# The expert router reads the raw residual, in four column strips

## What is computed

```python
def rmsnorm(x, w, eps=NORM_EPS):
    y = x * lax.rsqrt(jnp.mean(x * x, axis=-1, keepdims=True) + eps)
    return y * w
...
pg = jax.nn.softmax(hf @ w_group)          # hf = rmsnorm(h, norm_ffn_w), w_group (1024, 4)
gidx, gprob = jnp.argmax(pg), jnp.max(pg)
sub_all = jnp.einsum('btd,gde->btge', hf, w_sub)    # w_sub (4, 1024, 4)
vals, idx = lax.top_k(sub_of_group_gidx, 2)
w2 = softmax(vals) * gprob
hid = silu(hf @ w_gate[e]) * (hf @ w_up[e]) * gate ; out = hid @ w_down[e]
```

## Time and profile before

| what | value |
|---|---|
| median of 3 runs | 1477.9 us (1473.82, 1477.9, 1481.07) |
| profiled execution, its own time | 1483.33 us |
| its span, first to last instruction | 1481.5 us |
| TensorE busy | 1305.9 us, 88% |
| VectorE, ScalarE, GpSimd busy | 726.8, 410.8, 176.3 us |
| mean granted TensorE clock | 0.934 of full |
| MixOut and Experts of layer 0 | 375 to about 653 us of the span |
| MixOut and Experts of layer 1 | 1161.8 to about 1446 us of the span |

### The profile page before, as it was taken

How to read it: one execution, slowest core, us unless ns; L and a number is a source line. 1 busy time by engine, 2 the same in 40 slices (tenths; PEclk the granted TensorE clock), 3 DMA queues, 4 the chain that set the end, 5 groups by cost and what they waited for, 6 DMA issues and landing times. The chain is left out here.

```text
span 1481.5 us, 29946 instructions
## 1 busy us (share of the span) xinstructions
PE 1305.9 (88%) x11855; PEld 769.3 (52%) x11855; DVE 726.8 (49%) x1881; ACT 410.8 (28%) x1098; POOL 176.3 (12%) x247
## 2 busy tenths in 40 slices
PE   6999999998799998966999989858778699998897
PEld 3445555565366654534555545435554355755542
DVE  3445777676565311137353544368875565321123
ACT  3024445353210211133213121234546211121112
POOL 2002233222010000013021100100100001000002
PEclk9999999999898899987999999988998799799998
DMA  6150435223714899994455989899999622899925
GB/s 231 58 149 14 134 112 169 73 77 132 285 54 170 306 363 346 320 326 163 150 201 223 341 316 351 320 410 405 406 385 346 235 96 89 335 371 343 327 73 192
DMA packets 133278, 348.15 MB, mean 235 GB/s; under 512 B 22491, under 2 KB 52366, under 8 KB 124942
## 3 DMA queue, kind: packets, MB, share of 16 engines
q1 hardware_dynamic: 115906, 313.63, 59.3%
q0 software_dynamic: 4992, 17.83, 3.3%
q10 hardware_dynamic: 12236, 14.72, 3.0%
HBM read 302.61 MB, written 43.52 MB: 234 GB/s over the span
## 5 line engine op out<-in xcount | busy, mean ns | idle before, releaser
L409 PE MATMUL bank<-wring,xT 128*128 128x512 f32 x448 | 200.0, 601 | 0.0
L409 PEld LDWEIGHTS bank<-wring,xT 128*128 128x128 f32 x448 | 84.1, 192 | 100.2 <-issue 100.1
L1440 PE MATMUL bank<-wring,xT 128*128 128x512 f32 x256 | 120.1, 623 | 2.0 <-DVE xT L1360 2.0
L883 PE MATMUL bank<-xT,wring 128*128 128x512 f32 x256 | 113.5, 601 | 3.9 <-DVE hgrn_g L707 3.9
L2798 DVE STREAM_TRANSPOSE attn_k_pages<-attn_k_pages 128x1024 f32<-128x1024 f32 x64 | 77.6, 1232 | 46.5 <-DMA attn_k_pages<-cache_k 45.8
L883 PEld LDWEIGHTS bank<-xT,wring 128*128 128x128 f32 x256 | 48.7, 193 | 65.1 <-issue 59.6
L1440 PEld LDWEIGHTS bank<-wring,xT 128*128 128x128 f32 x256 | 49.6, 200 | 59.9 <-issue 59.8
L2798 DVE STREAM_TRANSPOSE wring<-wring 128x1024 f32<-128x1024 f32 x44 | 52.7, 1224 | 46.2 <-DMA wring<-cache_k 46.1
L785 DVE COPY_PREDICATED gla_att<-level_masks,bank 128x512 f32<-128x512 int32 x48 | 35.1, 731 | 71.8 <-PE bank L903 71.8
L2315 PE MATMUL bank<-xT,wring 128*128 128x512 f32 x128 | 56.9, 597 | 0.0
L903 PE MATMUL bank<-gla_qe,gla_ke 128*128 128x128 f32 x384 | 49.7, 285 | 0.0
(11 more groups left out here) (460 smaller groups left out, 2388.1 us busy)
## 6 DMA issues: line engine op xcount, KB each, us to landing
attn_k_pages<-cache_k SPq DMA_DIRECT2D x64, 512.0 KB, 7.7
wring<-cache_v SPq DMA_DIRECT2D x52, 512.0 KB, 7.7
attn_shared<-cache_v SPq DMA_DIRECT2D x44, 512.0 KB, 5.6
wring<-cache_k SPq DMA_DIRECT2D x44, 512.0 KB, 7.1
moe_wd<-moe_w_down SPq DMA_DIRECT2D x20, 1024.0 KB, 14.5
wring<-moe_w_gate SPq DMA_DIRECT2D x18, 1024.0 KB, 11.6
wring<-moe_w_up SPq DMA_DIRECT2D x18, 1024.0 KB, 15.8
wring<-a_w_in SPq DMA_DIRECT2D x16, 1024.0 KB, 10.6
```

Of the source, the lines that this page charges most:

```text
L409: last = nc.tensor.matmul(bank[:, :], xT[:, c, cols(t)], w[:, c, :], start=(c == 0), stop=(c == DC - 1))
L883: last = nc.tensor.matmul(bank[:, :], lhsT, k.xT[:, c, 0:SEQ], start=(c == 0), stop=(c == DC - 1))
L1440: last = nc.tensor.matmul(bank[:, :], k.xT[:, c, cols(t)], w[:, c, :], start=(c == 0), stop=(c == DC - 1))
```

## The change

The router's weights are scaled once per layer by the norm's weight (VectorE, in the second step), so that the router can read the residual h before it is normed: its transposes (1452) wait for the add, and take every eighth feature of the row (a step of 32 bytes), the order that the scaling used to make. The factor per token comes in the `pick`, where a copy becomes a multiply. The router's product is turned round: a chunk's router weights (padded to 32 columns) are the weights and the tokens move; four chunks stand beside each other in column strips of the array, and twice four chunks add up in them. ScalarE copies the four strips out of the bank, and one matmul with four stacked identities adds them and gives tokens by logits again. On TensorE this sum stands two chunks of the projection later, and in the last step the gather of the second tile follows it. After the loop, transposes, strips and sum of the last tile come ahead of the gather of the third. On VectorE, the last tile's copy to xT moves ahead of its inverse root and scaling. SyncE loads the norm's weight once more, by feature; GpSimd makes the padding and the stacked identities at the stage's start and waits for the scaled rows before it scatters.

```diff
--- before.py
+++ after.py
@@ -33,6 +33,7 @@
...
 EARLY, EXPERT_SLOTS = 3, 5
+STRIP = 32
 NB, STORES = 2, 6
...
@@ -1021,7 +1022,7 @@
...
         self.k, self.a, self.layer = k, a, layer
-        self.norm, self.router = sb("norm_w", [P, D]), sb("router", [P, DC, GROUPS + EXPERTS])
+        self.norm, self.strip_sum, self.strips = sb("norm_w", [P, D]), sb("strip_sum", [P, STRIP]), sb("strips", [P, P])
         by_width = lambda tile: tile[:, :, :].rearrange("p a b -> p (a b)").rearrange("p (w c f) -> p w c f", w=2, c=DC)
...
@@ -1029,6 +1030,7 @@
...
                   [late[:, i * part:(i + 1) * part].rearrange("p (c n) -> p c n", n=D) for i in range(EXPERT_SLOTS - EARLY)]
+        self.norm_column, self.router = k.cw[:, 3 + layer, :], sb("router", [P, DC, STRIP])
         self.gu_in = [sem(f"gate_up_landed{i}") for i in range(EXPERT_SLOTS)]
...
@@ -1038,6 +1040,7 @@
...
         by_feature = lambda x: x.rearrange("(p c) n -> p c n", c=DC)
+        sp.dma_start(self.norm_column, a["norm_ffn_w"][layer].rearrange("(p c) -> p c", c=DC)).then_inc(self.router_in, 16)
         sp.dma_start(self.router[:, :, 0:GROUPS], by_feature(a["moe_w_group"][layer])).then_inc(self.router_in, 16)
...
@@ -1078,14 +1081,18 @@
...
         self.big, self.more = sb("big", [P, MORE, E]), sb("more", [P, MORE])
...
 
-    def constants(self, pool, ch):
-
-        nc = self.nc
+    def constants(self, pool, ch, moe):
+
+        nc, quarter = self.nc, lambda j: self.k.ident[:, j * STRIP:(j + 1) * STRIP]
+        nc.gpsimd.memset(moe.router[:, :, GROUPS + EXPERTS:STRIP], 0.0).then_inc(self.padded, 1)
+        ch(nc.gpsimd.tensor_tensor(moe.strip_sum[:, :], quarter(0), quarter(1), ALU.add))
+        ch(nc.gpsimd.tensor_tensor(moe.strip_sum[:, :], moe.strip_sum[:, :], quarter(2), ALU.add))
+        nc.gpsimd.tensor_tensor(moe.strip_sum[:, :], moe.strip_sum[:, :], quarter(3), ALU.add).then_inc(self.padded, 1)
         nc.gpsimd.iota(self.count_i[:, :], pattern=[[1, CAP]], base=0, channel_multiplier=0).then_inc(self.made, 1)
...
@@ -1109,7 +1116,7 @@
...
 
-    def pick(self, dve, ch, i, t, bank):
+    def pick(self, dve, ch, i, t, bank, root):
 
...
@@ -1118,7 +1125,7 @@
...
         dve.wait_ge(self.logit, i + 1)
-        ch(self.nc.vector.tensor_copy(L, bank[r, t * 32:t * 32 + G + E]))
+        ch(TS(L, bank[r, t * STRIP:t * STRIP + G + E], root[r, :], None, ALU.mult))
         reduce_max(best[0], L[:, 0:G])
...
@@ -1247,10 +1254,10 @@
...
         (self.squared, self.summed, self.averaged, self.seeded, self.gated, self.turned, self.out_a, self.out_v, self.projected,
...
 
...
@@ -1272,10 +1279,11 @@
...
         routing = self.routing
-        routing.constants(pool, ch)
+        routing.constants(pool, ch, self.moe)
         self.k.order_n["gpsimd"] = ch.n
...
             pool.wait_ge(routing.slots_ready, i + 1)
+            pool.wait_ge(self.n_xs, i + 1)
             for j in range(TOPK):
...
@@ -1310,6 +1318,11 @@
...
             nc.scalar.activation(k.xT[:, half:DC, cols(t)], src, ACT.Copy).then_inc(self.n_out_a, 1)
+
+        def strips_out(i):
+            n, routing = rows(ORDER[i]), self.routing
+            act.wait_ge(routing.in_strips, i + 1)
+            nc.scalar.activation(self.moe.strips[:, 0:n], k.ps[6][:, HB - P:HB - P + n], ACT.Copy).then_inc(routing.strips_out, 1)
 
...
@@ -1322,9 +1335,11 @@
...
                 norm_out(i - 1)
+                strips_out(i - 1)
             squares(i, 1)
...
         norm_out(NT - 1)
+        strips_out(NT - 1)
 
...
@@ -1372,6 +1387,8 @@
...
             dve.wait_ge(self.n_mean, i + 1)
+            if i == NT - 1:
+                norm_out(i)
             dve.wait_ge(self.n_root, i + 1)
...
@@ -1385,6 +1402,15 @@
...
             nc.vector.tensor_copy(k.xT[:, 0:half, cols(t)], src).then_inc(self.n_out_v, 1)
+
+        def pick(i):
+            routing.pick(dve, ch, i, ORDER[i], logit_bank, self.mean[:, 5, ORDER[i]:ORDER[i] + 1])
+
+        def router_scaled():
+            dve.wait_ge(self.moe.router_in, 16 * (2 + GROUPS))
+            router = self.moe.router[:, :, 0:GROUPS + EXPERTS]
+            nc.vector.tensor_tensor(router, router, bcast(self.moe.norm_column, 2, [P, DC, GROUPS + EXPERTS]), ALU.mult)\
+                .then_inc(self.router_ready, 1)
 
...
@@ -1402,16 +1428,17 @@
...
             if i:
+                if i == 1:
+                    router_scaled()
                 norm_out(i - 1)
-                route(routing.pick, i - 1, logit_bank)
+                pick(i - 1)
             else:
...
         norm(NT - 1)
-        norm_out(NT - 1)
-        route(routing.pick, NT - 1, logit_bank)
+        pick(NT - 1)
         route(routing.slots, NT - 1, pos_bank)
...
@@ -1447,22 +1474,34 @@
...
             t = ORDER[i]
-            pe.wait_ge(self.n_xs, i + 1)
+            pe.wait_ge(self.added, 2 * i + 2)
+            by_chunk = k.h[0:rows(t), t, :].rearrange("p (q c) -> p c q", c=DC)
             for c in range(DC):
                 last = nc.tensor.transpose(k.ps[2 + c // half][:, (c % half) * P:(c % half) * P + rows(t)],
-                                           self.xs[0:rows(t), t, c * P:(c + 1) * P], k.ident[0:rows(t), 0:rows(t)])
+                                           by_chunk[:, c, :], k.ident[0:rows(t), 0:rows(t)])
             last.then_inc(self.n_turned, 1)
 
-        def logits(i):
+        def logit_strips(i):
+
             t = ORDER[i]
             if i == 0:
-                pe.wait_ge(moe.router_in, 16 * (1 + G))
+                pe.wait_ge(self.router_ready, 1)
+                pe.wait_ge(routing.padded, 2)
             pe.wait_ge(self.n_out_v, i + 1)
             pe.wait_ge(self.n_out_a, i + 1)
-            for c in range(DC):
-                last = nc.tensor.matmul(k.ps[6][0:rows(t), t * 32:t * 32 + G + E], k.xT[:, c, cols(t)], moe.router[:, c, :],
-                                        start=(c == 0), stop=(c == DC - 1))
-            last.then_inc(routing.logit, 1)
+            per = P // STRIP
+            for n in range(DC // per):
+                for j in range(per):
+                    last = nc.tensor.matmul(k.ps[6][j * STRIP:(j + 1) * STRIP, HB - P:HB - P + rows(t)], moe.router[:, n * per + j, :],
+                                            k.xT[:, n * per + j, cols(t)], start=(n == 0), stop=(n == DC // per - 1))
+            last.then_inc(routing.in_strips, 1)
+
+        def logit_sums(i):
+
+            t = ORDER[i]
+            pe.wait_ge(routing.strips_out, i + 1)
+            nc.tensor.matmul(k.ps[6][0:rows(t), t * STRIP:t * STRIP + G + E], moe.strips[:, 0:rows(t)], moe.strip_sum[:, 0:G + E],
+                             start=True, stop=True).then_inc(routing.logit, 1)
 
...
@@ -1479,9 +1518,10 @@
...
             pe.wait_ge(routing.selected, i + 1)
+            pe.wait_ge(self.n_xs, i + 1)
             return gather_tokens(nc, k.ps[0:2], self.xs, routing.select, ORDER[i], i == 0, i == NT - 1)
 
-        whole, first, second = range(DC), range(half), range(half, DC)
+        whole, first, second, third = range(DC), range(half), range(half, half + half // 2), range(half + half // 2, DC)
         turn(0)
...
@@ -1497,15 +1537,20 @@
...
             if i:
-                logits(i - 1)
+                logit_strips(i - 1)
             if i == NT - 1:
...
             project(i, 1, w[1], second)
+            if i:
+                logit_sums(i - 1)
+            if i == NT - 1:
+                gather(1)
+            project(i, 1, w[1], third)
         place(NT - 2)
-        gather(1)
+        norm_turn(NT - 1)
+        logit_strips(NT - 1)
+        logit_sums(NT - 1)
         gather(2)
-        norm_turn(NT - 1)
-        logits(NT - 1)
         gather(3)
...
```

More of the change, by code:

```diff
@@ L1080, in __init__ @@
         self.big, self.more = sb("big", [P, MORE, E]), sb("more", [P, MORE])
-        names = ("made", "cleared", "logit", "picked", "placed", "summed", "slots_ready", "selected", "counted", "sent", "gathered", "compared", "stepped", "to_exp",
+        names = ("made", "cleared", "padded", "in_strips", "strips_out", "logit", "picked", "placed", "summed", "slots_ready", "selected", "counted", "sent", "gathered", "compared", "stepped", "to_exp",
                  "exped", "blocks_ready")
-        (self.made, self.cleared, self.logit, self.picked, self.placed, self.summed, self.slots_ready, self.selected, self.counted,
+        (self.made, self.cleared, self.padded, self.in_strips, self.strips_out, self.logit, self.picked, self.placed, self.summed, self.slots_ready, self.selected, self.counted,
          self.sent, self.gathered, self.compared, self.stepped, self.to_exp, self.exped, self.blocks_ready) = (k.sem(f"{tag}_{n}") for n in names)
-    def constants(self, pool, ch):
-        nc = self.nc
+    def constants(self, pool, ch, moe):
[4 more added lines that the diff above has]
+        nc.gpsimd.tensor_tensor(moe.strip_sum[:, :], moe.strip_sum[:, :], quarter(3), ALU.add).then_inc(self.padded, 1)
```

(4 more changed lines are left out.)

## The result

The changed kernel took 1485.43 us in the median of 20 runs, the kernel before 1479.82 us in 20 runs beside it: ratio 1.004, 95% interval 1.0021 to 1.006. It is slower by 0.4%, or 5.6 us (3 to 9). The forecast was 0.26% faster. The profiled execution took 1484.43 us (span 1482.7), 0.1% under its median. That is only 1.1 us over the profiled execution of the kernel before (1483.33), so the rows of the two traces cannot hold the whole 5.6 us: they show where each path moved, and the times of the runs carry the sum.

A forecast was written before the change was run, and what follows sets the result against it. The prediction saw layer-end routing as the bound, with a path of transfers almost beside it. Limited by transfers, -1.5 us in layer 1 and -2.4 in layer 0 made -3.9: 1477.9 to 1474.0, range 1466 to 1485.

The forecast's parts named there:

- (a): Last tile's router no longer waits for the norm: pick 4.2 us earlier, 0.4 lost to gathers, routing line -3.8 in layer 1.
- (b): Router matmuls in column strips: 0.5 us against 1.86; with the gather moved in, the projection ends 0.9 us later.
- (c): Longer TensorE gap in the third pass brings a lower-clock spell: +1.0 us at the projection's end, bounds -1.3 and +2.5.
- (d): Transposing the residual loads weights at a 32-byte step: no penalty taken, upper bound +1.1 us per tile.
- (f): Transfers limit the gain: token reads land 2.5 us after the full stretch; expert 1's turn -1.5 us in layer 1, -2.4 in layer 0.
- The 3.8: Upper bound, in us, from the full transfer stretch's end to the first token read's landing; a read issued to idle engines.
- sign of being right: TensorE idle 1 to 2 us before the turn of expert 1's tokens, named as a wait on slots_x.
- the sign of being wrong: The projection ending more than 3 us later, or expert 1's turn following expert 0 with no wait.
- The shift is passed on, so that buys nothing: After expert 1's turn, weight loads follow TensorE's freed slots, passing the shift on; expert 5's earlier first weights gain nothing.
- the third rival: Transfers take the whole gain: reads need 3.8 us, clock spell doubles, +0.5 to +2 us per layer, 1479 to 1482; chance 0.2.
- The forecast's case: The routing gain arrives only as far as the transfers allow: 1471 to 1477 us; chance 0.37.

The follow-up runs named there:

- both undone: Changed kernel with the second tile's gather back behind the projection and TensorE's third-pass pause filled with unused matmuls; ratio to the kernel before 1.0001.
- the filled pause: Changed kernel with 13 unused matmuls of 224 columns where TensorE waits for the copy to xT in the third pass; ratio 0.9989.
- the second execution: Changed kernel, unedited, profiled and timed once more beside the kernel before; ratio 1.0034.
- the early weights: Changed kernel with expert 3's gate and up weights issued when the last tile's first half projection is done; ratio to the kernel before 0.9978.
- the waiting transposes: Changed kernel, but in the third pass alone the transposes wait for the scaling again; ratio to the kernel before 0.9999.
- the helps without the change: Kernel before, with expert 3's weights issued early and nine unused matmuls in the third pass's two gaps; ratio 0.9972.
- the best version: Changed kernel with the gather put back, TensorE's pause filled and expert 3's weights issued early; 1468.9 us, ratio to the kernel before 0.9914.

## Why the prediction was wrong, step by step

- **(a) was right.** The pick ends 5.2 us sooner after the projection in layer 1 and 5.8 in layer 0; 4.2 in absolute time with an add 0.7 to 0.9 later made 4.9 to 5.1. The 0.4 for the cold gathers was too small in layer 0: 32 instructions took 6.85 us at the lower clock (473.97 to 480.8), so the placement stood 1.8 us behind the pick's end (478.8).
- **(b) was right in its parts, too small in its sum.** 16 strip instructions take 0.64 us (0.5 forecast) at the upper clock and 1.08 at the lower, the two-instruction sum 0.24 to 0.4, and 0.62 at the lower clock in the third pass. The gather moved in takes 2.00 and costs the projection 1.8 (its own experiment). But the strips won only about 0.3 at the projection's end (71.9 with both undone, 72.15 to 72.2 before), where I had let them give back 1.1: without the clock the projection ends 1.5 later, not 0.9.
- **(c) failed in its size.** The stretch at 1.2 GHz grew from 3.4 to 6.8 us in both layers. Layer 0, where it had ended ahead of the fourth projection (7.13 in the earlier trace rows), now has it there too (8.21). I took +1.0 because the row near it cost 1.3; the filled pause gives 2.5 and 1.8, and the stated bound was 2.5. The projection ends 4.0 and 1.8 us later in place of 1.9 (4.05 and 2.55 in the second execution). In layer 1 the 1.8 looks like a hit, but there the kernel compared had its own costly stretch (8.40); its executions without one end at 72.2. Over three executions before and four after with TensorE's work unedited (the two kernels, the second profile and the kernels that moved weights alone) the end goes from 72.7 to 76.05 on average, 3.3 later per layer.
- **(d) was right.** Eight transposes with weights at a step of 32 bytes take 1.12 to 1.16 us where they took 1.09 to 1.11; only the 32-row tile shows more, 1.06 against 0.68. By the rule of the Trainium skill (SBUF — State Buffer, Door 1: The DMA port swizzle) crossing 16-byte lines has its penalty; it gives no size. For these loads the rows show at most 0.07 us per eight of the 128-row ones, not my upper bound of 1.1, and the measurement decides.
- **(f) failed, and here lies the sign.** I let the reads land 2.5 us after the full stretch, as if they flowed beside its end. But they are issued only once the last scatter has landed; that scatter, issued 4 to 5 us sooner, lands with the stretch all the same (8.84 us in place of 4.64), and the read takes its 3.65 after it. So where TensorE comes early enough to wait, the end of the projection fixes the turn, and not the routing; with the gather put back alone the routing still set it. The 3.8 stood in my bounds, and it was the right end, behind a stretch that itself ended later. The TensorE wait that I named as a sign of being right (1 to 2 us on slots_x) did come, 1.64 and 1.75: the path was right and its length wrong. And the sign of being wrong came too, a projection that ends more than 3 us later, in layer 0.
- **"The shift is passed on, so that buys nothing"** failed too. The experts behind the turn run on the same line of transfers: shifting 2.1 MB costs 0.6% with the turn in place. The kernel before stood on both lines at about the same time. The change shortened the one and lengthened the other, and the time follows the longer. In the changed kernel the line of transfers starts 5.8 us later over both layers (6.6 in the second execution), and 5.6 us were measured. That the two agree so closely is partly luck: by the averages under (c) it is 6.7. That all of the 5.6 goes by this line is worked out, not isolated. That starting it earlier wins the loss back is shown in two ways whose intervals lie apart from the 1.0021 to 1.006: the filled pause (0.9989; against the second set of runs, 1.0012 to 1.0055, it just overlaps) and the early weights (0.9978, apart from both), the latter with TensorE's program untouched. The gather put back (1.0018), the waiting transposes (0.9999) and both undone (1.0001) point the same way, but their intervals overlap it; and why both undone are not faster than the filled pause alone stays open.

What came true is the third rival, the transfers with the doubled clock spell, which I gave 0.2. Its 1479 to 1482 stood against 1477.9, where the measured ratio makes 1483.8, so even its own range was 2 us short: it took +2 per layer at most, and the projection's end alone brought 1.8 to 4.0. The forecast's case had looked likelier because I summed a gain of one line (2.8 us) and let the other line move by the small end of each unknown.

## What to carry to other kernels

Where two lines end within a microsecond of each other, a change must be summed on each from its own start, and what it does to the start of the other one (here a gather of 2 us and a slower clock ahead of the projection's end) counts in full. Test the slack by moving a known load (2.1 MB here) before believing it. A shortened line may show its worth only together with an edit that shortens the other: 1.004 for the change alone, 0.9978 with early weights, 0.9972 for the helps without the change, 0.9914 together.

## What was not expected of the hardware

Useless matmuls gained time. The profile's windows around the pause in layer 0 (columns as above) show the granted clock, last but two, at 0.50 right after it, while TensorE is busy throughout, and back at 1.00 only from 434:

```profile
425.00:428.00 3.00, 0.00 (x0) 0.00 (x0) 2.77 (x13) 1.70 (x4) 0.42 (x1) 0.80 0.00 0
428.00:431.00 3.00, 2.99 (x46) 2.43 (x50) 0.40 (x3) 0.28 (x1) 1.76 (x2) 0.50 0.52 195
431.00:434.00 3.00, 3.00 (x16) 1.32 (x9) 2.58 (x13) 0.00 (x0) 0.00 (x0) 0.56 0.39 160
434.00:437.00 3.00, 3.00 (x9) 1.33 (x8) 1.75 (x8) 0.93 (x3) 0.00 (x0) 1.00 0.00 0
```

With 5.19 us of matmuls in that pause the clock did not fall. Gathers go with either level: 32 gather instructions took 6.85 us in the changed kernel, where the clock fell to 0.50 within their first microsecond and stayed there, and 3.98 in the best version (layer 0), where it was 1.00. There it had risen again at 473.2, in the middle of a gather, with only these transposes and that gather run since it fell at 469.9:

```profile
469.90 1.97 PE L1480 MATMUL bank<-ident,h 128*128 128x128 f32 x8
471.66 2.74 PE L1234 MATMUL bank<-moe_select,hgrn_v 128*128 128x96 f32 x16
```

The same 16 take 2.00 at the upper level and 3.7 at the lower. Why it rose here and not in the changed kernel stays open. Beside a queue full of weights a scatter's time from issue to landing is not its own: 4.64 us and 8.84 us for the same 512 KB (128 rows of 4 KB), and 3.5 in the kernel before with early weights, where less stood in the queue.
